# Shorter clock products, an attention norm by blocks of rows, a last norm in two instructions a piece, and one more unit's low halves on GpSimd

## The reference

```python
h = rms_norm(h, norm_final)                       # end of the first block
h = layer_norm(x, ln_in_g, ln_in_b)               # norm 0 of the kernel
for l in range(2):
    proj = h @ w_in[l]
    ...                                           # two attentions, rms norms, concatenated
    mix = jnp.concatenate([oa, ob], axis=-1) @ w_o[l]
    h = layer_norm(ALPHA * h + mix, ln1_g[l], ln1_b[l])   # norms 1 and 3
    ffn = peer_ffn(h, ...)                        # 16384 experts: products with u and with v
    h = layer_norm(ALPHA * h + ffn, ln2_g[l], ln2_b[l])   # norms 2 and 4; norm 4 is the output

def layer_norm(x, g, b):
    mu = x.mean(-1, keepdims=True)
    var = jnp.square(x - mu).mean(-1, keepdims=True)
    return (x - mu) * lax.rsqrt(var + 1e-5) * g + b
```

## Time and profile before

| | |
|---|---|
| median of 3 runs | 2400.44 us (2398.69 to 2403.57) |
| the profiled execution's own time | 2400.53 us |
| its span in the profile | 2398.7 us |
| PE, PEld busy | 2347.3 us (98%), 2095.4 us (87%) |
| DVE, ACT, POOL busy | 1684.5 us (70%), 1301.3 us (54%), 573.9 us (24%) |
| granted clock, mean of the span | 0.996 |

### The profile page before, as it was taken

One profiled execution on the slowest core, in us unless ns is written; L12 is line 12 of the kernel. 1 busy time (PEld: TensorE's weight loads), 2 busy tenths in 40 slices (PEclk: granted clock), 3 DMA queues, 4 the chain that ended last, 5 costly groups with the idle time before them and its releaser, 6 DMA issues.

```text
span 2398.7 us, 42228 instructions
## 1 busy us (share of the span) xinstructions
PE 2347.3 (98%) x16485; PEld 2095.4 (87%) x16485; DVE 1684.5 (70%) x3068; ACT 1301.3 (54%) x2800; POOL 573.9 (24%) x440
## 2 busy tenths in 40 slices
PE   8999999999999999999999999999999999999998
PEld 7878989997899889999888887789989999888886
DVE  5745354446689778887776556869888888777556
ACT  6543345456564665545555555655665555555554
POOL 3626135555379000000000003378300000000000
PEclk9999999999999999999999999999999999999999
DMA  5311155554245556556776564245555656777554
GB/s 200 116 62 47 54 167 188 187 185 147 75 159 178 190 182 197 193 198 206 244 245 215 193 213 151 82 159 172 182 191 192 194 193 197 237 245 236 194 193 159
DMA packets 148150, 420.99 MB, mean 176 GB/s; under 512 B 15984, under 2 KB 49136, under 8 KB 147568
## 3 DMA queue, kind: packets, MB, share of 16 engines
q1 hardware_dynamic: 144080, 405.34, 51.9%
q0 software_dynamic: 2256, 8.99, 1.0%
q10 hardware_dynamic: 1616, 3.96, 0.4%
HBM read 400.40 MB, written 17.83 MB: 174 GB/s over the span
## 4 chain that ended last, share of the span: by engine, by line
PE 93%; DVE 3%; ACT 2%; POOL 1%; DMA 1%; issue 1%; ACTq 0%; DVEq 0%; SPq 0%
PE pb L465 92%; PE pb L474 1%; POOL lo L2635 1%; ACT arena L1334 1%; ACT hi L1322 0%; DVE arena L2284 0%; ACT arena L1528 0%; DMA cst<-in_consts 0%; DMA raw<-in_w_out 0%; DVE arena L1880 0%; DMA raw<-in_w_ffn_in 0%; DVE arena L1877 0%; DVE arena L2345 0%; ACT HT L1334 0%; ACT L1334 0%
## 5 line engine op out<-in xcount | busy, mean ns | idle before, releaser
L465 PE MATMUL pb<-HT,hi 128*128 128x256 f32 (+2 forms) x5232 | 1093.8, 302 | 3.9 <-POOL lo L2635 1.9
L1322 ACT CAST hi<-raw 128x512 fp32r<-128x512 f32 x1402 | 821.0, 620 | 372.8 <-PE pb L465 255.7
L465 PEld LDWEIGHTS pb<-HT,hi 128*128 128x128 f32 x5232 | 839.0, 191 | 42.6 <-issue 4.3
L465 PE MATMUL pb<-HT,lo 128*128 128x256 f32 (+1 forms) x2968 | 839.3, 283 | 0.0
L2635 POOL TENSOR_TENSOR lo<-raw,hi 128x512 fp32r<-128x512 f32 x384 | 525.3, 1390 | 437.1 <-ACT hi L1322 436.8
L1887 DVE TENSOR_TENSOR lo<-raw,hi 128x1024 fp32r<-128x1024 f32 x464 | 567.4, 1223 | 41.6 <-ACT hi L1322 41.4
L465 PEld LDWEIGHTS pb<-HT,lo 128*128 128x128 f32 x2968 | 566.6, 191 | 0.0
L465 PE MATMUL pb<-hi,WH 128*128 128x512 f32 x1112 | 433.2, 390 | 1.6 <-DVE WL L2569 1.1
L465 PE MATMUL pb<-lo,WH 128*128 128x512 f32 x1112 | 432.9, 389 | 0.0
L465 PE MATMUL pb<-hi,WL 128*128 128x512 f32 x1112 | 432.6, 389 | 0.0
L1334 ACT ACTIVATE arena<-pb 128x256 f32<-128x256 f32 (+2 forms) x216 | 82.4, 382 | 358.6 <-PE pb L465 355.6
(11 more groups left out here) (213 smaller groups left out, 2107.9 us busy)
## 6 DMA issues: line engine op xcount, KB each, us to landing
raw<-in_uT SPq DMA_DIRECT2D x256, 512.0 KB, 3.5
raw<-in_vT SPq DMA_DIRECT2D x256, 512.0 KB, 3.7
raw<-in_w_ffn_in SPq DMA_DIRECT2D x44, 512.0 KB, 3.8
raw<-in_wq SPq DMA_DIRECT2D x32, 512.0 KB, 3.5
wk<-kept SPq DMA_DIRECT2D x128, 128.0 KB, 3.5
raw<-in_w_in SPq DMA_DIRECT2D x24, 512.0 KB, 3.6
raw<-in_w_ffn_out SPq DMA_DIRECT2D x22, 512.0 KB, 4.4
raw<-in_w_gate SPq DMA_DIRECT2D x16, 512.0 KB, 3.2
```

The lines of the kernel that those rows point to most:

```text
L465: return e.matmul(o, l, r, start=start, stop=stop)
L1322: e.copy(u.hi[k], u.half[k]).then_inc(*s.up("hi", ("hi", g)))
```

## The change

1. The numbers of clock products ahead of the norms' transposes fall: norm 0 from 100 to 44, norms 1 and 3 from 40 to 20, norm 2 from 50 to 24.
2. Norms 1 and 3 go through `attention_norm`: statistics, root and reciprocal for each block by itself, with block 0's ahead of the last statistics, and (1,0) normalised by VectorE where ScalarE did it.
3. Norm 4 goes through `output_norm`: for each piece (x - mean) * gain in one instruction and times the reciprocal plus bias in a second, all on VectorE; `norm_root`'s work on ScalarE and GpSimd's two instructions go away, and the pieces go out in the order (0,0), (0,1), (1,0), (1,1).
4. The unit ("win", l, 0, 1) of both layers has both lo halves on GpSimd, where VectorE made the first.

```diff
@@ -174,7 +174,7 @@
             for g in range(4):
                 src = d["w_in_2"][l, g * 256:(g + 1) * 256, i * 512:(i + 1) * 512]
                 add(("win", l, i, g), src.rearrange("(k p) n -> p k n", p=128), dims=2,
-                    low=both if (i, g) < (0, 2) else pool)
+                    low=both if (i, g) < (0, 1) else pool)
         for hf, g in WO:
             src = d["w_o_2"][l, g * 256:(g + 1) * 256, hf * 512:(hf + 1) * 512]
             add(("wo", l, hf, g), src.rearrange("(k p) n -> p k n", p=128), dims=2, low=pool)
@@ -1015,8 +1015,8 @@
             ffn_out(j - 1)
     for (t, k), b in OUT.items():
         free[b] = [("z", t, k), ("sq2", t, k)]
-    warm(2, 50)
-    warm(3, 50)
+    warm(2, 22)
+    warm(3, 22)
 
     for l in range(2):
 
@@ -1175,8 +1175,8 @@
         out_last()
         emptied_by(OB, ("pre", l, 0))
         free[1] = [("hn", 2 * l + 1, 1, 1)]
-        warm(2, 20)
-        warm(3, 20)
+        warm(2, 10)
+        warm(3, 10)
 
 
         def first_queries():
@@ -1300,11 +1300,12 @@
                 for hf in range(2):
                     v_rows(j, u, hf, t)
         emptied_by({(0, k): OUTV[0, k] for k in range(2)}, ("pre", l, 1))
-        for k in range(2):
-            free[OUTV[1, k]] = [("hn", 2 * l + 2, 1, k)]
         if l == 0:
-            warm(2, 25)
-            warm(3, 25)
+            for k in range(2):
+                free[OUTV[1, k]] = [("hn", 2, 1, k)]
+        if l == 0:
+            warm(2, 12)
+            warm(3, 12)
 
 
 def scalar(e, s, m):
@@ -1779,7 +1780,13 @@
         for n in range(3, 8):
             take("wo", l, *WO[n])
         root_table()
-        norm_root(2 * l + 1, [m.XN[:, 1, 0:512], PB[OB[1, 1]][:, :]])
+        n = 2 * l + 1
+        for t in range(2):
+            w.wait_ge(*s.to("var_eps", n, t))
+            fn(sm[:, 102 + t:103 + t], sm[:, 100 + t:101 + t], ACT.Sqrt).then_inc(*s.up("roots", ("ln_root", n, t)))
+        w.wait_ge(*s.to("shift", n))
+        x = fn(m.Hv[:, 1, 512:1024], PB[OB[1, 1]][:, :], ACT.Identity, scale=sm[:, 103:104], bias=m.SHIFT)
+        x.then_inc(*s.up("norms_act", ("hn", n, 1, 1)))
 
 
         turned_biased(("exp", l), f"g1{l}", f"b1{l}", ("in", l), TURNS_EXP)
@@ -1850,8 +1857,11 @@
             if j + 1 < 128:
                 w_split(j + 1)
         root_table()
-        norm_root(2 * l + 2, [PB[OUTV[1, k]][:, :] for k in range(2)])
-    for t, k in HALVES:
+        if l == 0:
+            norm_root(2, [PB[OUTV[1, k]][:, :] for k in range(2)])
+    w.wait_ge(*s.to("var_eps", 4))
+    fn(sm[:, 102:104], sm[:, 100:102], ACT.Sqrt).then_inc(*s.up("roots", ("ln_root", 4)))
+    for t, k in ((0, 0), (0, 1), (1, 0), (1, 1)):
         cs = slice(k * 512, (k + 1) * 512)
         w.wait_ge(*s.to("y_out", t, k))
         e.dma_start(m.out[:, t, cs], m.Hv[:, t, cs]).then_inc(*s.up("out", ("out", t, k), by=16))
@@ -2195,7 +2205,7 @@
         if j:
             take("fout", j - 1)
 
-    def layer_norm(n, order, pieces, ready, src, extra=None):
+    def statistics(order, pieces, ready, src):
         def stats(t, k):
             w.wait_ge(*s.to(ready(t, k), t, k))
             e.bn_stats(m.ST6[:, t, k, :], src(t, k)).then_inc(*up("stats"))
@@ -2205,24 +2215,77 @@
                 pieces[t, k](t, k)
             if i:
                 stats(*order[i - 1])
-        stats(*order[3])
+        stats(*order[-1])
+
+    def means(*ts_):
         own()
-        for t in range(2):
+        for t in ts_:
             e.bn_aggr(m.MV[:, t, :], m.ST6[:, t, :, :]).then_inc(*up("stats"))
         own()
+
+    def root_of(n, extra=None):
         if extra is None:
             ts(sm[:, 100:102], m.MV[:, :, 1], 1e-5, None, A).then_inc(*up("stats", ("var_eps", n)))
         else:
             w.wait_ge(*s.to("mean_eps"))
             tt(sm[:, 100:102], m.MV[:, :, 1], extra, A).then_inc(*up("stats", ("var_eps", n)))
+
+    def inverse(n):
         w.wait_ge(*s.to("ln_root", n))
         e.reciprocal(sm[:, 102:104], sm[:, 102:104]).then_inc(*up("stats"))
         own()
+
+    def shift(n):
         stt(m.SHIFT, m.MV[:, 1, 0:1], -1.0, sm[:, 103:104], M, M).then_inc(*up("stats", ("shift", n)))
+
+    def scaled(n, t, k, src):
+        cs = slice(k * 512, (k + 1) * 512)
+        x = ts(m.Hv[:, t, cs], src, m.MV[:, t, 0:1], sm[:, 102 + t:103 + t], S, M)
+        x.then_inc(*up("norms", ("hn", n, t, k)))
+
+    def input_norm(n, order, pieces, ready, src, extra=None):
+        statistics(order, pieces, ready, src)
+        means(0, 1)
+        root_of(n, extra)
+        inverse(n)
+        shift(n)
         for k in range(2):
-            cs = slice(k * 512, (k + 1) * 512)
-            x = ts(m.Hv[:, 0, cs], src(0, k), m.MV[:, 0, 0:1], sm[:, 102:103], S, M)
-            x.then_inc(*up("norms", ("hn", n, 0, k)))
+            scaled(n, 0, k, src(0, k))
+
+    def attention_norm(n, pieces, ready, src):
+        def block_root(t):
+            means(t)
+            ts(sm[:, 100 + t:101 + t], m.MV[:, t, 1:2], 1e-5, None, A).then_inc(*up("stats", ("var_eps", n, t)))
+
+        def block_inverse(t):
+            w.wait_ge(*s.to("ln_root", n, t))
+            e.reciprocal(sm[:, 102 + t:103 + t], sm[:, 102 + t:103 + t]).then_inc(*up("stats"))
+            own()
+
+        statistics(HALVES[:3], pieces, ready, src)
+        block_root(0)
+        block_inverse(0)
+        scaled(n, 0, 0, src(0, 0))
+        statistics([(1, 1)], pieces, ready, src)
+        block_root(1)
+        scaled(n, 0, 1, src(0, 1))
+        block_inverse(1)
+        shift(n)
+        scaled(n, 1, 0, src(1, 0))
+
+    def output_norm(pieces, ready, src):
+        statistics([(0, 0), (0, 1), (1, 0), (1, 1)], pieces, ready, src)
+        means(0, 1)
+        root_of(4)
+        w.wait_ge(*s.to("bc", 4))
+        for i, (t, k) in enumerate([(0, 0), (0, 1), (1, 0), (1, 1)]):
+            cs, bs = slice(k * 512, (k + 1) * 512), slice(1024 + k * 512, 1536 + k * 512)
+            stt(m.FP[:, t, cs], src(t, k), m.MV[:, t, 0:1], m.BC2[:, cs], S, M).then_inc(*up("last"))
+            if i == 0:
+                inverse(4)
+            own()
+            x = stt(m.Hv[:, t, cs], m.FP[:, t, cs], sm[:, 102 + t:103 + t], m.BC2[:, bs], M, A)
+            x.then_inc(*up("last", ("y_out", t, k)))
 
     def gain_step(i, tag, bc, n):
 
@@ -2240,7 +2303,7 @@
         cs = slice(k * 512, (k + 1) * 512)
         tt(m.XN[:, t, cs], PB[OUT[t, k]][:, :], m.nfin[:, cs], M).then_inc(*up("norms", ("z", t, k)))
 
-    layer_norm(0, HALVES, {h: z for h in HALVES}, lambda t, k: "z", lambda t, k: m.XN[:, t, k * 512:(k + 1) * 512], sm[:, 62:64])
+    input_norm(0, HALVES, {h: z for h in HALVES}, lambda t, k: "z", lambda t, k: m.XN[:, t, k * 512:(k + 1) * 512], sm[:, 62:64])
     e.tensor_copy(m.IOT, C("iota").unsqueeze(2).to_broadcast([128, 128, 2])).then_inc(*up("setup"))
     own()
 
@@ -2444,7 +2507,7 @@
             return piece
 
         r = residual(m.XN, ("pre", l, 0), OB, ("wo_ps", l), ("in", l))
-        layer_norm(2 * l + 1, HALVES, {h: r for h in HALVES[:3]},
+        attention_norm(2 * l + 1, {h: r for h in HALVES[:3]},
                    lambda t, k: ("wo_ps", l) if (t, k) == (1, 1) else ("pre", l, 0),
                    lambda t, k: PB[OB[1, 1]][:, :] if (t, k) == (1, 1) else m.XN[:, t, k * 512:(k + 1) * 512])
         turned_biased(("exp", l), f"g1{l}", f"b1{l}", TURNS_EXP)
@@ -2608,17 +2671,12 @@
                 back += 1
             take("v", l, j)
         r = residual(m.FP, ("pre", l, 1), OUTV, ("v_out", l), ("exp", l))
-        layer_norm(2 * l + 2, [(0, 0), (0, 1), (1, 0), (1, 1)], {(0, k): r for k in range(2)},
-                   lambda t, k: ("v_out", l) if t else ("pre", l, 1),
-                   lambda t, k: PB[OUTV[1, k]][:, :] if t else m.FP[:, 0, k * 512:(k + 1) * 512])
-    w.wait_ge(*s.to("bc", 4))
-    for t, k in HALVES:
-        cs, bs = slice(k * 512, (k + 1) * 512), slice(1024 + k * 512, 1536 + k * 512)
-        if (t, k) != (1, 0):
-            w.wait_ge(*s.to("hn", 4, t, k))
-            tt(m.Hv[:, t, cs], m.Hv[:, t, cs], m.BC2[:, cs], M).then_inc(*up("last"))
-            own()
-            tt(m.Hv[:, t, cs], m.Hv[:, t, cs], m.BC2[:, bs], A).then_inc(*up("last", ("y_out", t, k)))
+        args = ({(0, k): r for k in range(2)}, lambda t, k: ("v_out", l) if t else ("pre", l, 1),
+                lambda t, k: PB[OUTV[1, k]][:, :] if t else m.FP[:, 0, k * 512:(k + 1) * 512])
+        if l == 0:
+            input_norm(2, [(0, 0), (0, 1), (1, 0), (1, 1)], *args)
+        else:
+            output_norm(*args)
 
 
 def gpsimd(e, s, m):
@@ -2732,11 +2790,6 @@
             elif j == 120 and l == 0:
                 w.wait_ge(*s.to("lent"))
                 tables(1)
-    w.wait_ge(*s.to("bc", 4))
-    w.wait_ge(*s.to("hn", 4, 1, 0))
-    tt(m.Hv[:, 1, 0:512], m.Hv[:, 1, 0:512], m.BC2[:, 0:512], M).then_inc(*s.up("last_pool", ("y_gain",)))
-    w.wait_ge(*s.to("y_gain"))
```

(1 more changed line is left out.)

## The result

The changed kernel takes 2391.3 us (median of 6 executions, 2388.0 to 2394.9) against 2400.5 us for the kernel before on the same chip (2398.7 to 2404.0): a ratio of 0.9958, 95% interval 0.9948 to 0.9968. The forecast was 2392.1. The profiled execution took 2390.88 us where that of before took 2400.53, 9.65 us less, and its span is 2389.1 us. Run again on another chip, with 10 executions, the same kernel had a median of 2392.6 and a ratio of 0.9957 (0.9945 to 0.9970).

A forecast was written before the change was run, and what follows sets the result against it. TensorE, busy 98% of the span, bounds the kernel; only the five norms could gain. 5.5 + 2.4 + 0.5 + 0.1 + 1.6 = 10.1 us off 2400.5 gives 2390.4, plus 1.7 for the clock: 2392.1, range 2388.5 to 2397.0.

The forecast's parts named there:

- Norm 0, 5.5: Ahead of norm 0's transposes: 44 clock products instead of 100 let transposes start earlier, gain 5.5 us, bounds 5.0 to 5.7.
- The cast: VectorE's cast of the iota table behind norm 0, until then covered by clock products, was expected to cost 0.1 us.
- The rival that the gain is not passed on: Behind norm 0: what follows waits for a weight load or hi part, so 5.5 us is lost, 2395.9; chance 0.07.
- Norm 2, 2.4: At norm 2: aggregate 2.25 us earlier, 24 products end before the data, transposes at 1469.45 instead of 1471.9, gain 2.4 us.
- The bound of 1.7: Lower bound of the gain at norm 2, 1.7 us, if GpSimd's two halves hold up a small VectorE instruction.
- The moved half, nothing: Second unit's lo half, slower on GpSimd, costs nothing: TensorE needs it over 3 us later; without that cover 0.6 us.
- Norms 1 and 3, 0.5 and 0.1: Block-wise norms: gain 0.5 us in layer 0, the middle of 1.0 and 0; 0.1 in layer 1, bounds -0.3 and 1.0.
- the late branch: At norms 1 and 3: VectorE just misses GpSimd's gap, (0,0) waits for its last half; layer 0 gain 0, worst -0.1.
- Norm 4, 1.6: VectorE's tail at norm 4: two instructions per piece, 0.75 us for the new one, end at 2394.7 against 2396.25, gain 1.6.
- The clock, one fall: TensorE's longer waits at the norms make the granted clock fall once more, likeliest at norm 3 or 1, costing 1.7 us.
- the sign I had given: What would show the clock's fall: PEclk below 1.00 behind some norm.
- The slower rival: Clock stays low for two stretches per fall, 3.4 us each, at four norms 13.6 us: 2404.0; chance 0.04.

## Why the prediction was right

The forecast was 10.1 us of gain less 1.7 for one fall of the clock, 8.4; the profile shows 10.8 less 1.56 and 9.65 in all, and the medians of before and after are 9.2 us apart in the first series and 11.1 in the second. By its steps:

- **Norm 0, 5.5.** Measured 5.62. The sums start at 536.59, and the moved half gives back 0.63 us, as forecast from VectorE's wait of 0.6. GpSimd's third half stayed covered. The cast, for which 0.1 was taken off, costs about 0.2: VectorE goes straight from it to the first chunk (544.16), and from (1,0) being ready (543.57) to the first product it is 2.18 us where norm 2, which has no cast, needs 1.98. The rival that the gain is not passed on fell: from the first product behind norm 0 to the last ahead of norm 1 it is 103.34 us in both kernels.
- **Norm 2, 2.4.** Measured 2.59. The aggregate starts 1.15 us behind the last product, forecast 1.16 from norm 4's row. The bound of 1.7, GpSimd holding up a small instruction, was escaped by the place: the addition to 128x2 began at 1461.23, only 0.17 us before GpSimd's halves ended (1461.40), and took 0.20 in place of 0.17.
- **The moved half, nothing.** Shown by itself: ratio 0.9996. Both 0.64 and 2.22 us hang on it once the products are short.
- **Norms 1 and 3, 0.5 and 0.1.** Measured 0.46 and 0.44. The mechanism was the one named, (0,0) lengthened until a half of GpSimd ends, and it took the late branch in both layers, by a hair: VectorE asked at 649.56, and the second of GpSimd's two halves had begun near 649.49 (648.23 and half of 2.51). For that branch I had said 0 to -0.1. The step that was mis-sized is the end of (0,0): I let its work begin when GpSimd's half was over, but the row ends only 0.28 us behind that (651.02 against 650.74). From the end of that half to (1,0) being ready it is 2.50 us (650.74 to 653.24), where I had 2.9, and the half ended 1.65 us behind the start of the last real product where in before it ended 1.79 behind it. So the 0.5 of norm 1, a middle of two branches, is right by luck. And the comparison that I didn't make matters more: the short products alone would have given 1.44.
- **Norm 4, 1.6.** Measured 1.67; an instruction takes 0.75, as assumed, and a pair 1.45 against the assumed 1.43.
- **The clock, one fall.** One in the first profile, two in the second, at 1.4 to 1.6 us each against 1.7. Only the latter two are behind norms 1 and 3, where I had expected one; the sign I had given, PEclk below 1.00 behind some norm, is missing from the first profile, so that its count of one and its time agree with the forecast is partly luck. Where the clock falls differs between executions of one kernel. The seven profiles with stretches of 4.9 to 5.95 us at norms 1 and 3 have no fall at these fourteen norms, the two of the changed kernel with 6.2 have two at four. Whether the longer wait causes the falls is not shown: stretches of 5.9 us, hardly shorter, had none at four norms. Why one fell in the attention of layer 1, where all other profiles kept the clock, stays open. The slower rival's falls of double length exist, two of four once all products are out, but they cost 2.0 and 2.1 us and not 3.4, and with the products that the change leaves no profile has one behind a norm. TensorE: Matmul & The Clock Gate in the Trainium skill ("What's actually happening") says that activity lifts the clock out of a slow default; these runs agree, since with the products out it fell behind every norm.

On which of VectorE's instructions wait for GpSimd the prediction had only "reads and writes SBUF". The runs draw the line elsewhere. Held were the normalisation of 128x512 (1.46 us) and the product of two columns in SCALAR_TENSOR_TENSOR (1.19). Held too was TENSOR_SCALAR on 128x2: in before, in the change at norm 2 and with norms 1 and 3 made whole it took 0.34, 0.20 and 0.23 us in place of 0.17 and each time ended 0.02 to 0.03 us behind GpSimd's last half. Not held were TENSOR_SCALAR on 128x1 (0.15 to 0.21), the reciprocal of 128x1 (0.16), aggregates, and statistics. So for TENSOR_SCALAR the difference between one column and two matters, and the norm by blocks, whose additions are to one column, avoids this wait. No run moved GpSimd's halves away from these instructions; that they are what holds is read from where the waits end. GPSIMD Engine Reference in the Trainium skill (section 8, Key points) names as contending the instructions in a mode that takes two ports and those with two SBUF inputs; the second kind is the shift of two columns, and the change from 1.19 to 0.21 us by taking a column as TENSOR_SCALAR's scalar agrees with it.

## What to carry to other kernels

Put in front of a late, critical instruction only what no other engine can hold up; an early start for something that waits on a shared path costs more than it brings. Judge a small instruction by its kind and its operands, and not by its duration alone. Size clock padding to end where the data come, not to zero: here the padding that ended before the data cost nothing and its removal lengthened the span by 6.2 us, and edits that shorten the data's path show their worth only once the padding over them is cut.

## What the runs showed of the hardware

- A SCALAR_TENSOR_TENSOR of 128x1 needs 0.16 us alone and 1.18 to 1.19 us beside a GpSimd TENSOR_TENSOR of 128x512; the same product as TENSOR_SCALAR with a column for its scalar needs 0.21.
- A TENSOR_SCALAR of 128x2 beside that GpSimd instruction took 0.34 us in place of 0.17 and ended with it, where one of 128x1 took 0.15 in its midst.
- Six falls of the clock for 3.4 us cost 1.25 to 1.99 us each, two of 6.8 us cost 2.0 and 2.1, read from stretches that differ by 0.4 to 0.8 us without a fall. One came behind a half-idle stretch at which the same work kept its clock in all twelve other profiles. Without clock products it fell behind all four norms, after waits of 1.58 to 4.87 us ahead of the transposes.
